# Four pieces, not three, of the next GEMM begun inside the layer norms of a one-core transformer kernel, and another order of the last norm

## The chip, the cores and the metric

One core of a Trainium2 chip. The metric is the device time of one execution in microseconds, median of several runs. The engines are TensorE (PE in the profile, its weight loads PEld), VectorE (DVE), ScalarE (ACT), GpSimd (POOL) and SyncE (SP), which here only issues transfers.

## The reference

A block of one mixture layer is followed by two post-norm layers, 512 tokens by 1024 features, in float32. The change lies in the layer norms of the latter:

```
def layernorm(x, g, b):
    mu = mean(x); var = mean((x - mu) ** 2)
    return (x - mu) * rsqrt(var + LN_EPS) * g + b

def hybrid_layer(x, ...):                  # twice
    ...                                    # fox attention and retention -> mixed
    x = layernorm(ALPHA * x + mixed @ w_out, ln1_g, ln1_b)
    hid = square(relu(x @ w_ff1))
    return layernorm(ALPHA * x + hid @ w_ff2, ln2_g, ln2_b)
```

So there are four norms. Norms 1 and 3 (the first of each layer) are followed by the GEMM with w_ff1, norm 2 by the projections of the second layer (w_in), norm 4 by the output.

## The kernel before, in words

Activations lie transposed: features on the 128 partitions in 8 tiles k, the 512 tokens along the free axis. H holds the residual stream. Each GEMM operand is split into a high and a low part (Phi and Plo, Qhi and Qlo, wh and wl), and each product is three matmuls: high by high (L298), low by high (L300), high by low (L301). A GEMM of one piece (128 output features) is 8 tiles k, 24 matmuls of 512 columns, or twice 24 of 256 columns where it is done by token halves. Results go to PSUM banks 0 to 3 in turn; the norms' sums use banks 4 and 5.

**Weights.** A slab of two pieces is loaded by SyncE (L229) into one of two stages. prepare() takes the next piece and splits it: ScalarE writes the high part (L269), VectorE the low part (L270), into a slot of a ring: slots 0 to 3, and after widen() also 4 to 6, which lie over buffers that attention uses; narrow() gives these back. When both pieces of a stage are split, the next slab's load is issued. piece() hands out the next piece and prepares ahead; piece(1) prepares nothing more than it needs.

**Order.** Every engine has one in-order queue, written by V.op (VectorE), A.op (ScalarE), PE.op and SP.op in program order. An op waits for the tokens that it is given; a token is a count of its engine's semaphore, so a wait for an op is also one for all that stands before it in that queue.

**The norm.** Norm.tile(j) adds tile j of H to accq (L1164) and, against a rough centre cB, takes deviations (L1180), squares (L1187) and their sum acc2 (L1196). The last three tiles, 5 to 7, are made by last_three() in two token halves, A_ (tokens 0 to 255) and B_ (256 to 511). part(p, hf, ks) does the matmuls of tile 5+p for half hf; if ks ends with 7 it evacuates them (L1273, or L1277 without the factor alpha) and calls norm.late(j, sl): add to accq (L1202), whose token becomes norm.acc, and deviate(). norm.add() adds pending squares.

For each half, mean() is a float32 matmul of accq with a matrix of 1/1024 (L1217, two matmuls), a copy by ScalarE into muB (L1219), and the difference to cB and its square (L1220, L1221). minus(k) subtracts muB (L1226). scale() is a matmul of acc2 (L1231), the variance (L1233), and ln and exp on ScalarE (L1235, L1236). times(k) multiplies by rB (L1241), lets ScalarE apply gain and bias (L1244) and, if a GEMM follows, write Phi (L1247); lows(k) writes Plo (L1253). head(half, ks) does the matmuls of the next GEMM's first pieces, each on its bank, tile by tile as they come.

The order before is: tiles 5, 6 and 7 of half A; 9 matmuls of tile 5's half B; A's mean; 6 matmuls; A's scale; 9 matmuls; tile 6's and tile 7's half B, with A's times() and lows() put between; then the head with three pieces for half A, with B's mean and scale inside, and for half B. Two pieces are prepared ahead of half B's head. Behind the head the three banks are evacuated, and the GEMM goes on with its fourth piece. In norm 2 the pieces are those of fq0, fk0 and fq1, evacuated by Heads.queries (L602, L603) and keys (L617, L618); the fourth, fk1, is a GEMM of its own, and a thin GEMM of 8 output features (gemm_thin) follows it. In norm 4 no GEMM follows: out_half() has SyncE write finished tiles to the output, four at a time for half A (512 KB), two for half B (256 KB).

## Time and profile before

| | |
|---|---|
| Runs | 2123.3, 2123.97, 2124.76 us; median 2123.97 |
| The profiled execution | 2123.57 us |
| Its span, first to last instruction | 2121.8 us |
| Mean granted clock of TensorE | 0.995 |
| Norm 1, from tile 5 to the end of its head | 1089 to 1132 us |
| Norm 2 | 1449 to 1491 us |
| Norm 3 | 1728 to 1772 us |
| Norm 4, to the end | 2089 to 2122 us |

Every time in the views is in us from the span's start, for this one execution. In a timeline a row is an instruction, or several of the same line in a row (x3), with start and duration; in brackets stands the time for which its engine had nothing to do before it, and what released it. Durations of one engine's instructions overlap: of 256-column ones on VectorE each takes 0.42 us. A matmul's shape such as 128x256 gives the columns.

### The profile page before, as it was taken

To read this page: it belongs to the slowest core of one execution; us is meant where nothing else is said; L and a number is where in the kernel's file an instruction comes from. 1 tells how busy PE (TensorE), PEld (TensorE's weight loads), DVE (VectorE), ACT (ScalarE), POOL (GpSimd) and SP (SyncE) were. 2 spreads that over 40 slices of the span, in tenths; PEclk is the share of its full clock that TensorE was granted. 3 is DMA by queue.
4 is the path that set the end of the run, shared out by engine and by line. 5 is a ranking of instruction groups with operands and counts; after the bars stand their busy time and mean duration, and the time that the engine had idled before them with its cause. 6 is when DMAs were issued, how large, how long until landed. Compare 5 with 4: busy or idle time off the path is not lost. (4 is left out here: it accounts for less than half of the span.)

```text
span 2121.8 us, 24498 instructions
## 1 busy us (share of the span) xinstructions
PE 2055.1 (97%) x9660; PEld 1691.6 (80%) x9660; DVE 1101.9 (52%) x1795; ACT 939.3 (44%) x1513; POOL 149.4 (7%) x207
## 2 busy tenths in 40 slices
PE   8999999999999999999999999999999999999997
PEld 6888778888888888777688888888777688888886
DVE  5655556565343443576486333337676476333336
ACT  5664334335232332565557243244565347243343
POOL 0000000000000000353000000000353000000000
PEclk9999999999999999999999999999999999999999
DMA  7332213333322332632323332330632323333321
GB/s 236 95 105 64 77 60 99 121 98 120 119 91 88 100 99 61 179 100 75 114 80 102 99 103 95 100 99 21 199 91 83 114 80 100 100 99 100 99 80 40
DMA packets 201519, 211.38 MB, mean 100 GB/s; under 512 B 7803, under 2 KB 181115, under 8 KB 201404
## 3 DMA queue, kind: packets, MB, share of 16 engines
q1 hardware_dynamic: 194544, 194.13, 29.2%
q0 software_dynamic: 6352, 15.24, 2.8%
q8 instruction: 77, 1.26, 0.3%
q10 hardware_dynamic: 508, 0.43, 0.1%
q14 instruction: 38, 0.31, 0.0%
HBM read 194.55 MB, written 8.95 MB: 96 GB/s over the span
## 5 line engine op out<-in xcount | busy, mean ns | idle before, releaser
L298 PE MATMUL ps<-Phi,wh 128*128 128x512 f32 (+1 forms) x1208 | 481.1, 398 | 18.9 <-DVE Plo L448 8.7
L301 PE MATMUL ps<-Phi,wl 128*128 128x512 f32 (+1 forms) x1208 | 459.3, 380 | 0.1
L300 PE MATMUL ps<-Plo,wh 128*128 128x512 f32 (+1 forms) x1208 | 458.4, 380 | 0.0
L269 ACT ACTIVATE wh<-stage 128x1024 fp32r<-128x1024 f32 (+2 forms) x253 | 261.5, 1041 | 183.9 <-PE ps L301 167.1
L270 DVE TENSOR_TENSOR wl<-stage,wh 128x1024 fp32r<-128x1024 f32 x250 | 304.6, 1223 | 66.2 <-ACT wh L269 58.5
L298 PEld LDWEIGHTS ps<-Phi,wh 128*128 128x128 f32 x1208 | 228.4, 189 | 67.0 <-issue 19.6
L301 PEld LDWEIGHTS ps<-Phi,wl 128*128 128x128 f32 x1208 | 227.7, 188 | 44.7 <-DVE wl L270 0.8
L300 PEld LDWEIGHTS ps<-Plo,wh 128*128 128x128 f32 x1208 | 228.5, 189 | 40.8 <-issue 4.1
L298 PE MATMUL ps<-Qhi,wh 128*128 128x512 f32 (+1 forms) x680 | 256.2, 377 | 0.8 <-DVE Qlo L445 0.8
L301 PE MATMUL ps<-Qhi,wl 128*128 128x512 f32 (+1 forms) x680 | 254.4, 374 | 0.0
L300 PE MATMUL ps<-Qlo,wh 128*128 128x512 f32 (+1 forms) x680 | 254.4, 374 | 0.0
L445 DVE TENSOR_TENSOR Qlo<-f,Qhi 128x512 fp32r<-128x512 f32 x96 | 66.5, 693 | 238.8 <-ACT Qhi L444 238.8
L1120 DVE TENSOR_TENSOR H<-H,ps 128x512 f32<-128x512 f32 x72 | 49.5, 687 | 222.6 <-PE ps L301 222.6
L298 PE MATMUL ps<-Qhi,wxh 128*128 128x512 f32 (+1 forms) x408 | 150.7, 369 | 0.0
L300 PE MATMUL ps<-Qlo,wxh 128*128 128x512 f32 (+1 forms) x408 | 148.9, 365 | 0.0
L301 PE MATMUL ps<-Qhi,wxl 128*128 128x512 f32 (+1 forms) x408 | 148.8, 365 | 0.0
L298 PEld LDWEIGHTS ps<-Qhi,wh 128*128 128x128 f32 x680 | 128.1, 188 | 25.3 <-ACT Qhi L444 1.6
L300 PEld LDWEIGHTS ps<-Qlo,wh 128*128 128x128 f32 x680 | 128.1, 188 | 23.6 <-issue 1.0
L301 PEld LDWEIGHTS ps<-Qhi,wl 128*128 128x128 f32 x680 | 128.0, 188 | 22.7
L269 ACT ACTIVATE wxh<-stage 128x1024 fp32r<-128x1024 f32 x86 | 89.7, 1051 | 109.2 <-PE ps L301 104.3
L298 PE MATMUL ps<-Phi,wxh 128*128 128x512 f32 (+1 forms) x336 | 129.0, 384 | 0.0
L300 PE MATMUL ps<-Plo,wxh 128*128 128x512 f32 (+1 forms) x336 | 129.0, 384 | 0.0
(301 smaller groups left out, 2921.5 us busy)
## 6 DMA issues: line engine op xcount, KB each, us to landing
stage<-in_w_ff SPq DMA_DIRECT2D x64, 1024.0 KB, 5.4
stage<-in_w_in SPq DMA_DIRECT2D x39, 1024.0 KB, 5.3
stage<-in_w_up SPq DMA_DIRECT2D x16, 1024.0 KB, 5.3
stage<-in_w_down SPq DMA_DIRECT2D x16, 1024.0 KB, 5.2
stage<-in_w_in SPq DMA_DIRECT2D x30, 512.0 KB, 5.3
stage<-in_w_out SPq DMA_DIRECT2D x12, 1024.0 KB, 5.2
stage<-in_w_bg SPq DMA_DIRECT2D x4, 1024.0 KB, 5.4
vrev<-H SPq DMA_DIRECT2D x2, 2048.0 KB, 14.9
```

Source lines behind the costliest of these rows:

```text
L269: t_hi = A.op(lambda e: e.activation(hi, src, ACT.Copy), st_landed[n, part], w_free[u], sem=s_whi)
L270: t_lo = V.op(lambda e: e.tensor_tensor(lo, src, hi.bitcast(F32), ALU.subtract), st_landed[n, part], t_hi, w_free[u], sem=s_wlo)
L298: PE.op(lambda e: e.matmul(o, hi[:, k, c], x.hi[:, kx, tok], start=first, stop=False), t_hi, t_x or x.t[kx], list(waits), signal=False)
L300: PE.op(lambda e: e.matmul(o, hi[:, k, c], x.lo[:, kx, tok], start=False, stop=False), signal=False)
L301: return PE.op(lambda e: e.matmul(o, lo[:, k, c], x.hi[:, kx, tok], start=False, stop=last), t_lo, sem=s_wpe, signal=last)
L445: t2 = V.op(lambda e: e.tensor_tensor(lo, src, hi.bitcast(F32), ALU.subtract), t1, t_src, x.free, after)
L1120: t_h[j] = V.op(lambda e: e.tensor_tensor(H[:, j, :], H[:, j, :], o, ALU.add), t, t_h[j])
```

## The change

In last_three():

- The fourth piece of the next GEMM is prepared right behind tile 7's half A and norm.add(), and the head has four pieces. narrow() comes after it.
- A's mean comes after all of tile 5's half B (24 matmuls), A's scale after 4 of 8 tiles k of tile 6's half B. times(), lows() and minus() of both halves are dealt out anew.
- Half B's head goes tile by tile over the four pieces up to k = 3, then piece by piece over k = 4 to 7. If last_wide is not set, each bank is evacuated behind its piece; with last_wide (norm 2) all four are evacuated behind the last product.
- The GEMM goes on with its fifth piece: ff() begins at 4, and in norm 2 the thin GEMM follows at once.
- In norm 4, tile 7's half B is not added to accq and acc2. mean(7) and scale(True) let TensorE add it, by a second float32 matmul into the same bank each. Of times(), tiles 2 and 5 get gain and bias from VectorE (tensor_scalar) and not from ScalarE. B's operations are woven into A's, and A's last tile is finished later.

```diff
-            def late(self, j, sl):
+            def late(self, j, sl, summed=True):
-                self.acc = V.op(lambda e: e.tensor_tensor(accq[:, sl], accq[:, sl], H[:, j, sl], ALU.add),
-                                t_h[j], self.acc)
+                if summed:
+                    self.acc = V.op(lambda e: e.tensor_tensor(accq[:, sl], accq[:, sl], H[:, j, sl], ALU.add),
+                                    t_h[j], self.acc)
                 self.deviate(j, sl)
...
-            def mean(self):
+            def mean(self, rest=None):
...
+                if rest is not None:
+                    t = PE.op(lambda e: e.matmul(banks[4][:, sl], onec[:, :], H[:, rest, sl], start=False, stop=True),
+                              t_h[rest])
...
-            def scale(self):
+            def scale(self, rest=False):
...
+                while rest and n.pending:
+                    _, _, s, t_s = n.pending.pop()
+                    t = PE.op(lambda e, s=s: e.matmul(banks[5][:, sl], onec[:, :], s[:, sl], start=False, stop=True), t_s)
...
+                    if not self.keep and k in (2, 5):
+                        self.fin[k] = V.op(lambda e, k=k, g=g, b=b: e.tensor_scalar(
+                            H[:, k, sl], d8[:, k, sl], g, b, ALU.mult, ALU.add), t)
+                        continue
...
-                norm.late(j, sl)
+                norm.late(j, sl, then)
...
+            part(2, 0, range(8))
+            norm.add()
+            if nxt:
+                prepare()
             if last_wide:
                 narrow()
-            part(2, 0, range(8))
-            norm.add()
-            part(0, 1, range(3))
+            part(0, 1, range(8))
             A_.mean()
             A_.minus(0, 1, 2, 3)
-            part(0, 1, (3, 4))
+            part(1, 1, range(4))
             A_.scale()
             A_.minus(4, 5, 6, 7)
-            part(0, 1, (5, 6, 7))
+            part(1, 1, range(4, 8))
             A_.times(0, 1)
+            if not nxt:
+                norm.add()
+                part(2, 1, range(8), False)
+                A_.times(2, 3)
+                B_.mean(7)
+                B_.minus(0)
+                B_.scale(True)
+                A_.times(4)
+                B_.minus(1, 2, 3, 4, 5)
+                A_.times(5, 6)
+                B_.minus(6, 7)
+                B_.times(0)
+                A_.times(7)
+                out_half(0, A_.fin)
+                for k in range(1, 8):
+                    B_.times(k)
+                    out_half(1, B_.fin, k)
+                return
             A_.lows(0)
-            part(1, 1, range(8))
-            for k in range(2, 5):
-                A_.times(k)
-                A_.lows(k - 1)
+            A_.times(2)
+            A_.lows(1)
+            A_.times(3)
             part(2, 1, range(8))
             norm.add()
+            A_.lows(2)
+            A_.times(4)
...
+            four = [(piece(1), next_bank()) for _ in range(4)]
...
             head(A_, (0, 1))
+            A_.lows(3)
+            A_.times(5)
             B_.mean()
-            A_.times(5)
             A_.lows(4)
-            B_.minus(0, 1)
+            B_.minus(0, 1, 2)
+            A_.times(6)
+            A_.lows(5)
             head(A_, (2, 3))
             B_.scale()
-            A_.times(6)
-            A_.lows(5)
-            B_.minus(2, 3, 4)
+            B_.minus(3, 4)
             A_.times(7)
-            A_.lows(6, 7)
+            A_.lows(6)
+            B_.minus(5, 6, 7)
+            A_.lows(7)
             head(A_, (4, 5, 6, 7))
...
+            head(B_, range(4))
+            for ((i, w), b), ev in zip(four, nxt):
+                for k in range(4, 8):
+                    t = step(B_, k, i, w, b)
+                P.free = t
+                release(i, t)
+                if not last_wide:
                     free[b] = ev(banks[b][:, :], t)
+            for ((i, w), b), ev in zip(four, nxt if last_wide else ()):
+                free[b] = ev(banks[b][:, :], t)
```

## Rows read from the trace of the kernel before

**Rows 1.** The page, busy time, share of the span and instructions of each engine.

```profile
PE 2055.1 (97%) x9660; PEld 1691.6 (80%) x9660; DVE 1101.9 (52%) x1795; ACT 939.3 (44%) x1513; POOL 149.4 (7%) x207
```

**Rows 2.** Waits of TensorE: line, for what, us in total, times, longest.

```profile
PE ps L1217 <- DVE accq L1202: 8.9, 6, 2.1
...
PE ps L298 <- ACT H L1244: 4.7, 3, 1.6
...
PE ps L298 <- DVE Plo L1253: 3.1, 8, 0.6
```

**Rows 3.** Timeline, TensorE, norm 1: start, us, what, [idle before <-releaser].

```profile
1098.18 0.28 PE L298 MATMUL ps<-Qhi,wxh 128*128 128x256 f32 x1
...
1100.28 0.70 PE L1217 MATMUL ps<-accq,onec 128*128 128x256 f32 x2 [0.86 <-DVE accq L1202]
...
1113.58 0.70 PE L1217 MATMUL ps<-accq,onec 128*128 128x256 f32 x2 [1.55 <-DVE accq L1202]
...
1123.92 0.35 PE L298 MATMUL ps<-Phi,wh 128*128 128x256 f32 x1 [1.58 <-ACT H L1244]
```

**Rows 4.** Timeline, ScalarE and VectorE, norm 1.

```profile
1100.60 0.42 ACT L1187 ACTIVATE sq<-d 128x256 f32<-128x256 f32 x1 [1.62 <-DVE d L1180]
...
1106.37 0.60 ACT L1244 ACTIVATE H<-d,prm 128x256 f32<-128x256 f32 x1
...
1088.65 3.50 DVE L270 TENSOR_TENSOR wl<-stage,wh 128x1024 fp32r<-128x1024 f32 x3
...
1101.78 1.42 DVE L1226 TENSOR_TENSOR d<-H,muB 128x256 f32<-128x256 f32 x4
```

**Rows 5.** Stretches: from:to, busy us (matmuls) of PE first, PEclk third from last.

```profile
222.00:226.00 4.00, 1.60 (x9) 1.06 (x8) 3.54 (x6) 1.25 (x3) 0.00 (x0) 1.00 0.11 8
...
1620.00:1627.00 7.00, 2.01 (x9) 1.44 (x9) 4.97 (x11) 3.05 (x6) 3.15 (x4) 1.00 0.00 0
...
1739.80:1743.30 3.50, 3.50 (x13) 3.14 (x13) 2.60 (x8) 1.22 (x3) 0.00 (x0) 0.51 0.00 0
```

**Rows 6.** Timeline, VectorE and TensorE, norm 3, first mean.

```profile
1737.71 1.22 DVE L270 TENSOR_TENSOR wl<-stage,wh 128x1024 fp32r<-128x1024 f32 x1 [0.59 <-ACT wh L269]
1738.85 0.41 DVE L1273 SCALAR_TENSOR_TENSOR H<-H,ps 128x256 f32<-128x256 f32 x1
...
1739.78 1.16 PE L1217 MATMUL ps<-accq,onec 128*128 128x256 f32 x2 [2.09 <-DVE accq L1202]
```

**Rows 7.** Timeline, norm 2: a square, the end of its head, evacuations, a split.

```profile
1459.16 0.42 ACT L1187 ACTIVATE sq<-d 128x256 f32<-128x256 f32 x1 [1.88 <-DVE d L1180]
...
1491.06 0.28 PE L301 MATMUL ps<-Phi,wxl 128*128 128x256 f32 x1
1491.18 0.40 PE L298 MATMUL ps<-Phi,wh 128*128 128x512 f32 x1
...
1496.66 0.40 PE L333 MATMUL ps<-Phi,wh 128*40 128x512 f32 x1
...
1492.01 1.41 DVE L603 SCALAR_TENSOR_TENSOR f0qs<-ps,f0qs 64x512 fp32r<-64x512 f32 x2 [0.99 <-ACT f0qs L602]
...
1496.33 1.06 ACT L269 ACTIVATE wh<-stage 128x1024 fp32r<-128x1024 f32 x1 [1.26 <-DMA stage<-in_w_in]
```

**Rows 8.** Timeline and DMA, norm 4; last, one line's instructions (ns min/median/max).

```profile
2108.18 0.42 DVE L1277 TENSOR_TENSOR H<-H,ps 128x256 f32<-128x256 f32 x1
...
2114.63 2.77 DVE L1241 TENSOR_TENSOR d<-d,rB 128x256 f32<-128x256 f32 x8
...
2115.08 4.04 ACT L1244 ACTIVATE H<-d,prm 128x256 f32<-128x256 f32 x8 [0.74 <-DVE d L1241]
...
out_T<-H SPq DMA_DIRECT2D x2, 512.0 KB, 3.0
out_T<-H SPq DMA_DIRECT2D x4, 256.0 KB, 2.2
...
L875 DVE TENSOR_SCALAR x_z<-x_z,prm x2: 474/474/475, 868.3 to 1505.0; 8x512 f32<-8x512 f32 x2
```

More of the change, by code:

```diff
@@ L1213, in __init__ @@
                 self.y, self.fin, self.sub = {}, {}, {}
-            def mean(self):
+            def mean(self, rest=None):
                 sl, n = self.sl, self.n
-                t = PE.op(lambda e: e.matmul(banks[4][:, sl], onec[:, :], accq[:, sl], start=True, stop=True),
+                t = PE.op(lambda e: e.matmul(banks[4][:, sl], onec[:, :], accq[:, sl], start=True, stop=rest is None),
                           n.acc, free[4])
+                if rest is not None:
+                    t = PE.op(lambda e: e.matmul(banks[4][:, sl], onec[:, :], H[:, rest, sl], start=False, stop=True),
+                              t_h[rest])
                 self.t_m = free[4] = A.op(lambda e: e.activation(muB[:, sl], banks[4][:, sl], ACT.Copy), t, n.start)
@@ L1227, in minus @@
                                      self.t_m, t_h[k], self.n.d[k])
-            def scale(self):
+            def scale(self, rest=False):
                 sl, n = self.sl, self.n
-                t = PE.op(lambda e: e.matmul(banks[5][:, sl], onec[:, :], acc2[:, sl], start=True, stop=True),
+                t = PE.op(lambda e: e.matmul(banks[5][:, sl], onec[:, :], acc2[:, sl], start=True, stop=not rest),
                           n.acc2, free[5])
+                while rest and n.pending:
+                    _, _, s, t_s = n.pending.pop()
+                    t = PE.op(lambda e, s=s: e.matmul(banks[5][:, sl], onec[:, :], s[:, sl], start=False, stop=True), t_s)
                 t = V.op(lambda e: e.tensor_tensor(qB[:, sl], banks[5][:, sl], qB[:, sl], ALU.subtract), t, self.q)
@@ L1302, in last_three @@
             A_.lows(0)
-            part(1, 1, range(8))
-            for k in range(2, 5):
-                A_.times(k)
-                A_.lows(k - 1)
+            A_.times(2)
+            A_.lows(1)
+            A_.times(3)
             part(2, 1, range(8))
             norm.add()
-            if nxt:
-                two = [(piece(1), next_bank()) for _ in range(3)]
-            def head(half, ks):
-                for k in ks if nxt else ():
-                    for (i, w), b in two:
-                        t = product(banks[b][:, half.sl], w, k, slice(0, 128), P, k, k == 0, k == 7, free[b],
-                                    tok=half.sl, t_x=half.sub[k])
-                        if k == 7 and half is B_:
-                            P.free = t
-                            release(i, t)
-                return t if nxt else None
+            A_.lows(2)
@@ L1322, in last_three, with step @@
+            A_.times(4)
+            four = [(piece(1), next_bank()) for _ in range(4)]
+            def step(half, k, i, w, b):
+                return product(banks[b][:, half.sl], w, k, slice(0, 128), P, k, k == 0, k == 7, free[b],
+                               tok=half.sl, t_x=half.sub[k])
+            def head(half, ks):
+                for k in ks:
+                    for (i, w), b in four:
+                        step(half, k, i, w, b)
             head(A_, (0, 1))
+            A_.lows(3)
@@ L1337, in last_three @@
-            B_.minus(5, 6, 7)
             B_.times(0)
@@ L1341, in last_three @@
                 B_.lows(k - 1)
-                if nxt is None:
-                    out_half(1, B_.fin, k)
             B_.lows(7)
-            if nxt:
-                prepare()
-                prepare()
+            prepare()
+            prepare()
             for k in range(8):
                 t_h[k] = [A_.fin[k], B_.fin[k]]
-                P.t[k] = [A_.sub.get(k), B_.sub.get(k)]
+                P.t[k] = [A_.sub[k], B_.sub[k]]
             rb_free[0] = B_.r
             sq_free[:] = [norm.acc2, norm.acc2]
-            if nxt:
-                t = head(B_, range(8))
-                for (_, b), ev in zip(two, nxt):
+            head(B_, range(4))
[5 more added lines that the diff above has]
+                if not last_wide:
                     free[b] = ev(banks[b][:, :], t)
+            for ((i, w), b), ev in zip(four, nxt if last_wide else ()):
+                free[b] = ev(banks[b][:, :], t)
         fring = [pair_ring("f0", g0 + 54), pair_ring("f1", g0 + 28)]
@@ L1622, in build @@
             last_three(norm, alpha, V_LN1G + 8 * L, V_LN1B + 8 * L,
-                       [lambda o, t, j=j: up(j, o, t) for j in range(3)])
+                       [lambda o, t, j=j: up(j, o, t) for j in range(4)])
             norm = None
-            for j in ff(up, alpha, 3, 5):
+            for j in ff(up, alpha, 4, 5):
                 if norm is None:
```

6 lines of the change are left out of this document (2 added, 4 removed).

## The prediction

> **What bounds the kernel now.** I read the page first: TensorE is busy for 2055.1 of 2121.8 us [rows 1], so only time in which it waits can be won, and every new wait is paid in full. The waits of TensorE, longest first, show what the four norms cost it [rows 2]: 8.9 us before the mean sums (L1217), 4.7 us before the second half's first GEMM products, 3.1 us in eight waits of at most 0.6 for low parts of P in the first half's head. The timeline of norm 1 places the long ones [rows 3]: 0.86 us before the first half's mean at 1100.28, 1.55 before the second half's at 1113.58, 1.58 before the second half's head at 1123.92. Start to start each is some 0.2 us longer; with three of the eight norm 1 loses 6.2 us. Norms 2 and 3 repeat it: norm 2 has no first wait, norm 3 has 2.09 us there [rows 6], after a weight split on VectorE. Norm 4 ends the kernel.
>
> Reading VectorE and ScalarE [rows 4], the norm is a chain on two in-order queues. Four VectorE operations of 256 columns take 1.42 us, so one passes every 0.335 us; an operation that needs the one before it starts 0.45 us after it. A weight split takes ScalarE 1.06 us [rows 7] and holds VectorE for 1.14 us a piece (three in 3.50). A 256-column matmul passes every 0.119 us, a 512-column one every 0.228 (24 from 1491.18 to 1496.66) [rows 7].
>
> **Part 1, order around the first half's mean, norms 1 to 4.** Before, A_.mean() stands behind 9 products of the second half of tile 5. Now it stands behind all 24 and their late(). late() evacuates that half and adds it to accq, and norm.acc then names this later add. The matmul of A_.mean() waits for norm.acc, so it now waits for a sum that it doesn't need. Before those two VectorE operations stands the new prepare(). By hand, norm 1: the last square of half A starts at 1100.60 [rows 4]; the ScalarE split follows 0.33 later and takes 1.05; VectorE's split starts at 1102.0 and passes in 1.14; evacuation 0.45 and add 0.43 end at 1104.0, mean at 1104.1. TensorE has been free since 1098.18 + 24 x 0.119 = 1101.0 [rows 3]. The wait grows from 1.1 to 3.1 us. Norm 2 by the same steps from its square at 1459.16 [rows 7]: mean at 1462.6 against TensorE free at 1460.6, 2.1 us where there was none. Norm 3, from its mean at 1739.78 and so 3.8 later: 4.2 us [rows 6]. Norm 4 has no prepare(): mean at 2101.8, 1.2 us.
>
> **Part 2, the fourth piece in the head.** A's mean at 1104.1 gives VectorE its first input 1.15 later, as now from 1100.28 to one operation before 1101.78 [rows 3, 4]. Mean and variance step and 8 subtractions are 10 x 0.335: 1108.6. Tile 6 takes 2.0 (evacuation 0.45, add, deviation and two sums 4 x 0.335, 0.2 for ScalarE's square): 1110.6. Then times 0.45, ScalarE's scale-and-shift 0.63, its copy 0.45, low part 0.43, and 0.14 until TensorE starts: the first product of head A at 1112.7. TensorE arrives at 1104.1 + 0.53 + 0.53 (mean and variance matmuls) + 48 x 0.119 = 1110.8. That is a wait of 1.9 us where there was 0.8. Head A then has 96 products (11.4 us) in place of 72. It covers the second half's chain nearly: the 1.8 before B's mean goes, and of the others (0.4, 0.6, 1.8) I get 0.3, 0.1, 0.3, 0.3 within head A and 0.4 before head B, by passing the new order through the two queues with these durations. Sum of norm 1: waits 6.2 before, 3.1 + 1.9 + 1.4 = 6.4 after; half B's head ends at 1137.8, against 1123.92 + 72 x 0.119 = 1132.5 and 5.5 more for the piece that was a GEMM of its own. The half-width products cost 48 x 0.119 against 24 x 0.228, 0.2 more, and are in it. The same order applied to the old kernel gives 6.6 of waits where the trace has 6.2, so the change of norm 1 is -0.4 to +0.4; I take -0.1. Norms 2 and 3 have the same queue work and come out the same, -0.2 each. The fourth split is no new work: it moves from the end of the head, where VectorE waited for ScalarE at every tile, to where VectorE is the limit, and that is what eats the gain. It also issues the next slab's load on SyncE some 29 us earlier; SyncE's queue holds nothing else there and the other stage is full already, so nothing waits for it. Behind norm 2 the split at 1496.33, which waited 1.26 us for its load, is no longer on a load's heels [rows 7]; TensorE did not wait for it, so that is worth 0. Without the moved split these steps give 1.1 (norm 2) to 1.9 us gained.
>
> VectorE as a strict queue is the rule that speaks against this place. The trace shows it in norm 3: the split at 1737.71 holds back the evacuation at 1738.85, which needs nothing of it [rows 6]. The Trainium skill, "TensorE: Matmul & The Clock Gate", section "Architectural detail", says that ScalarE and VectorE are strict first-in first-out; by that rule the evacuation behind the moved split can't pass it, and the trace agrees.
>
> **Part 3, the clock.** In norm 3 the granted clock fell behind the wait: 0.51 from 1739.8 to 1743.3, which is 1.2 GHz, and 13 matmuls ran there, where 3.5 us hold 29 at 0.119 [rows 5]. It fell likewise behind 1620 to 1627, with TensorE busy 2.01 of 7 us, and not behind the 2.4 us without work near 222 us. Norm 1's new 3.1 us lie among these cases, norm 3's 4.2 beyond them. A fall costs nothing to 1.7 us (half of 3.4); half of it is covered, since head A waits for VectorE anyway, but mean, tile 6 and its evacuation come later. I take 1.1 for norm 1, and 0.9 for norm 3, whose old fall cost little (it lay on VectorE's chain). Norm 2 at 2.1: nothing taken, 1.2 as the upper bound.
>
> **Part 4, the bank behind norm 2.** Before, fq0, fk0 and fq1 were evacuated behind the head while a GEMM of 24 full products on the fourth bank ran: the last head product started at 1491.06 and the next at 1491.18 [rows 7]. Now all four banks are in the head, last_wide evacuates behind its last product, and the thin GEMM comes next, on fq0's bank. It waits for two ScalarE copies, and for two VectorE operations that end at 1492.01 + 1.41 = 1493.42 [rows 7]; TensorE would go on at 1493.55, 2.35 us late. Nothing else stands there to cover it. Bounds: 0, were another bank next in the round of four, and 3.1, were one more 0.7 us operation ahead on VectorE. In norms 1 and 3 the evacuations go out piece by piece in the head: 0. The head's new order needs half B's tile 7 after 4 x 12 + 9 products, 6.8 us; low parts come every 0.95 us, the last after 6.6: 0 as well, 0.3 at most.
>
> **Part 5, the last norm.** Half B's last tile is ready at 2101.8 + 0.53 + 0.53 + 48 x 0.119 + 0.2, evacuated at 2108.9, 0.7 later than now [rows 8]. Then mean(7)'s copy stands on ScalarE behind A_.times(3), which VectorE reaches after deviation, times(2), its new tensor_scalar and times(3), at 2110.5: copy at 2111.4, variance on VectorE at 2112.8. Behind it stand 22 VectorE operations before the last times, 22 x 0.335 and three dependent steps at 0.12 more: 2120.5, against 2114.63 + 7 x 0.335 = 2116.97 now. Three of A's times that now stand before the last evacuation come after it, and four scale-and-shifts join VectorE (ScalarE's 8 of 4.04 us are then no longer the limit, VectorE is). Last scale-and-shift ends 2121.7 against 2119.12: +2.6. Output: A's second 512 KB go out at 2118.5, not 2114.4, so 1536 KB leave from there; 512 KB land 3.0 and 256 KB 2.2 us after their issue [rows 8], so each 256 KB takes 0.8 or a little less and 1.4 is latency: 4.6 + 1.4, 2124.5, against 2119.15 + 2.2. So +2.6 to +3.1. The new tensor_scalar has no row at 128 x 256; bounds 0.24 (half of the 8 x 512 one of 474 ns) and 0.42 (a tensor_tensor of that width); that 8 x 512 one, with a column of prm, is the nearest in kind; it took 474 ns, where full-width tensor_tensors take 0.7 [rows 7], so some 0.3, and I take +2.8.
>
> For that operation the Trainium skill, "VectorE: DVE Perf Modes", section "Walkthrough: the 8-slice pipeline in each mode", says that fp32 tensor_scalar between SBUF tiles makes two results a cycle. With its 151 fixed cycles at 0.96 GHz an estimate from that page is 0.29 us, and the tail would be +2.7. The row of 474 ns agrees in kind; no run here shows the form itself.
>
> **Sum.** Norm 1: -0.1 + 1.1; norm 2: -0.2 + 2.35; norm 3: -0.2 + 0.9; norm 4: +2.8. Together +6.65, from the profiled execution's 2123.57 (span 2121.8, 1.8 around it) to 2130.2. The median of the runs is 0.4 above that execution: 2130.5.
>
> **Rivals.** (a) The clock falls too in norm 2 or behind the bank wait: +1.2 and +1.7. For it: 2.09 us sufficed in norm 3. Against: 2.4 us near 222 us did not. 2132 to 2133.5. (b) The moved split is covered: if VectorE had idle time there, norms 1 to 3 would gain 1.9, 1.1 and 1.9 and with the tail and the bank come to +0.25: 2124.2, no difference. Against: its operations follow each other without a gap there, as at 1101.78 [rows 4]. (c) Faster: the place is B's mean and B's head. If both lose their waits, 1.8 and 1.8 in three norms, and A's mean is not held back, -10.8 against +5.15 for bank and tail gives 2118.3; it decides if head A's first product comes less than 0.8 us after TensorE is free. Against: part 1's token. (d) The tail alone turns, as ScalarE's 4.04 us of scale-and-shifts fall by a quarter: -1.0 in place of +2.8, 2126.7.
>
> **How the numbers follow.** Forecast 0.62 (2127.5 to 2132, with (d) at its edge); (a) 0.18; (b) 0.12; (c) 0.08. 0.2%, about what a measurement of this kernel can tell from no change, is 4.2 us: under 2119.8 faster, over 2128.2 slower. Faster 0.06; same 0.16, which is (b) and the low edge of the forecast; slower 0.78. The range leaves out (c), most of (b) and the far end of (a): 2125.5 to 2133.5.
>
> **What would show it.** In the new profile: idle before L1217 near 3, 2, 4 and 1 us, released by an accq add of the second half, with one VectorE split ahead of it; head A's first product 1.5 to 2.3 us late; near nothing before B's mean; a wait of 2 to 2.5 us of the thin GEMM's first product on a VectorE evacuation; two falls of the clock in norms 1 and 3; from last evacuation to last scale-and-shift 12.8 us, now 10.9. Wrong if A's mean starts with no wait, if the B-half waits stay, or if the tail after the last GEMM product is not longer.

## The result: 0.46% slower, and the profile of the changed kernel

Median of five runs 2133.84 us (2131.38 to 2135.22) against 2123.3 us for the kernel before on the same chip. The ratio of the means (2133.35 and 2123.68) is 1.0046, with a 95% interval of 1.0031 to 1.006. The profiled execution took 2131.38 us, the shortest of the five, with a span of 2129.5 us and a mean granted clock of 0.993 (before: 0.995).

The page, busy time by engine, and TensorE's waits (line, for what, us, times, longest):

```profile
PE 2059.9 (97%) x9736; PEld 1696.9 (80%) x9736; DVE 1102.3 (52%) x1797; ACT 936.0 (44%) x1509; POOL 149.5 (7%) x207
```

```profile
PE ps L1219 <- DVE accq L1203: 9.7, 4, 4.1
...
PE ps L298 <- ACT H L1256: 5.1, 3, 1.8
...
PE ps L333 <- DVE f0qs L603: 2.2, 1, 2.2
```

TensorE has 76 instructions more than in [rows 1] and is busy 4.8 us more, and the span is 7.7 longer. The 8.9 us before the mean sums [rows 2] are now 9.7, but in 4 waits of up to 4.1 where there were 6 of up to 2.1: all stand before half A's mean, none before B's. The eight waits for low parts of P (0.2 to 0.6 us each) have gone from the list. The three for ScalarE's H (L298, 4.7 us then) stood before head B and now stand before head A, and the thin GEMM (L333) has a new one.

TensorE's timeline, the long waits of norm 1 (mean, head A), norm 2 (mean), the thin GEMM behind it, norm 3 and norm 4 (mean):

```profile
1100.47 0.28 PE L301 MATMUL ps<-Qhi,wxl 128*128 128x256 f32 x1
1103.58 0.70 PE L1219 MATMUL ps<-accq,onec 128*128 128x256 f32 x2 [2.83 <-DVE accq L1203]
...
1112.23 0.36 PE L298 MATMUL ps<-Phi,wh 128*128 128x256 f32 x1 [1.78 <-ACT H L1256]
...
1462.02 0.70 PE L1219 MATMUL ps<-accq,onec 128*128 128x256 f32 x2 [1.88 <-DVE accq L1203]
...
1498.28 0.62 PE L333 MATMUL ps<-Phi,wh 128*40 128x512 f32 x1 [2.21 <-DVE f0qs L603]
...
1747.58 0.80 PE L1219 MATMUL ps<-accq,onec 128*128 128x256 f32 x1 [4.06 <-DVE accq L1203]
...
2106.23 0.70 PE L1219 MATMUL ps<-accq,onec 128*128 128x256 f32 x2 [0.97 <-DVE accq L1203]
```

What stands before the first of them, VectorE's timeline:

```profile
1100.56 0.42 DVE L1196 TENSOR_TENSOR acc<-acc,sq 128x256 f32<-128x256 f32 x1 [0.48 <-ACT sq L1187]
1101.51 1.23 DVE L270 TENSOR_TENSOR wxl<-stage,wxh 128x1024 fp32r<-128x1024 f32 x1 [0.52 <-ACT wxh L269]
1102.65 0.41 DVE L1285 SCALAR_TENSOR_TENSOR H<-H,ps 128x256 f32<-128x256 f32 x1
1103.10 0.42 DVE L1203 TENSOR_TENSOR accq<-accq,H 128x256 f32<-128x256 f32 x1
```

The last product of tile 5's second half starts at 1100.47; half A's last add was over before that. The mean starts at 1103.58, right behind the add at 1103.10, which is half B's and which it doesn't need. Ahead of that add stands the moved split (1101.51, passed by 1102.65).

Stretches (from:to, busy us and matmuls of PE first, PEclk third from last):

```profile
1103.00:1106.00 3.00, 2.42 (x17) 2.31 (x18) 2.10 (x7) 1.22 (x3) 0.00 (x0) 1.00 0.61 182
1497.90:1501.30 3.40, 3.02 (x8) 1.35 (x9) 3.25 (x6) 3.26 (x7) 2.64 (x5) 0.51 1.05 389
1624.20:1634.40 10.20, 6.93 (x22) 5.26 (x20) 4.99 (x9) 2.33 (x5) 0.46 (x1) 0.50 0.01 2
1747.10:1750.50 3.40, 2.92 (x11) 2.75 (x12) 2.01 (x6) 1.22 (x3) 0.00 (x0) 0.50 0.70 218
```

The clock kept its upper level, 2.4 GHz, behind norm 1's wait of 2.83 us. It fell to 1.2 GHz behind the thin GEMM's wait and behind norm 3's, and at 1624.2, in the retention part, it stayed low for 10.2 us; the kernel before had 3.4 us there, at 1627.2.

The end (VectorE, ScalarE, output DMA, and one line's instructions with ns min/median/max):

```profile
2113.44 0.42 DVE L1289 TENSOR_TENSOR H<-H,ps 128x256 f32<-128x256 f32 x1
...
2114.69 0.41 DVE L1253 TENSOR_SCALAR H<-d,prm 128x256 f32<-128x256 f32 x1
2115.01 0.42 DVE L1249 TENSOR_TENSOR d<-d,rB 128x256 f32<-128x256 f32 x1
...
2124.73 0.75 DVE L1249 TENSOR_TENSOR d<-d,rB 128x256 f32<-128x256 f32 x2
...
2115.98 0.36 ACT L1224 ACTIVATE muB<-ps 128x256 f32<-128x256 f32 x1
...
2125.18 1.09 ACT L1256 ACTIVATE H<-d,prm 128x256 f32<-128x256 f32 x2 [0.36 <-DVE d L1249]
...
out_T<-H SPq DMA_DIRECT2D x2, 512.0 KB, 3.0
out_T<-H SPq DMA_DIRECT2D x4, 256.0 KB, 3.2
...
L1253 DVE TENSOR_SCALAR H<-d,prm x4: 414/414/414, 2114.7 to 2124.4; 128x256 f32<-128x256 f32 x4
```

From the last evacuation (2113.44) to the end of the last scale-and-shift (2125.18 + 1.09) it takes 12.83 us; [rows 8] give 10.94. The output's last 256 KB are there 2.85 us after that, 2.24 before. The new tensor_scalar takes 414 ns and lets the next operation pass after 0.32 (2114.69 to 2115.01), as a tensor_tensor of that width does.

One more row, from the retention part (TensorE):

```profile
1670.12 0.95 PE L1582 MATMUL ps<-x_rqk 128*128 128x256 f32 x4 [1.74 <-DVE x_IT L1585]
```

It waits for VectorE, and VectorE for a load of decay factors (x_dec). The load landed 12.0 us after its issue, 10.9 before. The same place in the kernel before, and a wait of that kernel between the thin GEMM and norm 3 that has all but gone in the changed one (no wait over 0.3 us for x_fvv is left):

```profile
1525.17 0.47 PE L298 MATMUL ps<-Phi,wh 128*128 128x512 f32 x1 [1.40 <-DVE x_fvv L773]
...
1666.12 0.95 PE L1547 MATMUL ps<-x_rqk 128*128 128x256 f32 x4 [0.64 <-DVE x_IT L1550]
```

Set beside the trace of before, stretch by stretch: up to the end of norm 1's fourth piece -0.65 us; on to the thin GEMM's start +2.26; on to norm 3 +2.42; in norm 3 +0.44; from there to the end +3.28. Together +7.75. The third of them, matmul by matmul: the fall behind the bank wait +1.39; then -1.68, at that wait for x_fvv; the low clock at 1624 +1.56; the load +1.11.

Of the first -0.65, norm 1 has only -0.17. These are its first half-width product and the first full-width one behind its head, in the kernel before and in the changed kernel:

```profile
1089.55 0.28 PE L298 MATMUL ps<-Qhi,wxh 128*128 128x256 f32 x1
1138.09 0.39 PE L298 MATMUL ps<-Phi,wxh 128*128 128x512 f32 x1
...
1089.08 0.28 PE L298 MATMUL ps<-Qhi,wxh 128*128 128x256 f32 x1
1137.45 0.40 PE L298 MATMUL ps<-Phi,wxh 128*128 128x512 f32 x1
```

That is 48.54 and 48.37 us. The other 0.47 lies ahead of norm 1, where both kernels do the same.

### The profile page after: what moved, and what is told of

Its sections match the earlier page's. It is cut to its first block and busy times, and to the rows that moved or that the text cites. A ratio compares the mean times of both kernels' runs of the same rounds, so it can differ in the third digit from the quotient of the medians.

```text
span 2129.5 us, 24654 instructions
## 1 busy us (share of the span) xinstructions
PE 2059.9 (97%) x9736; PEld 1696.9 (80%) x9736; DVE 1102.3 (52%) x1797; ACT 936.0 (44%) x1509; POOL 149.5 (7%) x207
## 5 line engine op out<-in xcount | busy, mean ns | idle before, releaser
L298 PE MATMUL ps<-Phi,wh 128*128 128x512 f32 (+1 forms) x1200 | 477.3, 398 | 15.3 <-DVE Plo L448 9.0
L298 PEld LDWEIGHTS ps<-Phi,wh 128*128 128x128 f32 x1200 | 227.0, 189 | 64.4 <-issue 24.1
L298 PE MATMUL ps<-Qhi,wh 128*128 128x512 f32 (+1 forms) x680 | 256.9, 378 | 0.8 <-DVE Qlo L445 0.8
L298 PE MATMUL ps<-Qhi,wxh 128*128 128x512 f32 (+1 forms) x408 | 149.8, 367 | 0.0
L298 PEld LDWEIGHTS ps<-Qhi,wh 128*128 128x128 f32 x680 | 128.0, 188 | 25.2 <-ACT Qhi L444 1.6
L300 PE MATMUL ps<-Plo,wxh 128*128 128x512 f32 (+1 forms) x368 | 136.4, 371 | 0.0
L298 PE MATMUL ps<-Phi,wxh 128*128 128x512 f32 (+1 forms) x368 | 136.4, 371 | 0.0
## 6 DMA issues: line engine op xcount, KB each, us to landing
vrev<-H SPq DMA_DIRECT2D x2, 2048.0 KB, 12.8
```

The costliest lines, as they stand in the source:

```text
L298: PE.op(lambda e: e.matmul(o, hi[:, k, c], x.hi[:, kx, tok], start=first, stop=False), t_hi, t_x or x.t[kx], list(waits), signal=False)
L300: PE.op(lambda e: e.matmul(o, hi[:, k, c], x.lo[:, kx, tok], start=False, stop=False), signal=False)
```

## The experiments

Theory: the order around A's mean and the split ahead of it (part 1), VectorE's queue (part 2), the clock (3), the bank (4) and the tail (5) add up as predicted. Rivals are named with each run. They were measured in four groups, each on a chip of its own with the kernel before beside it (medians 2122.9 to 2124.0); a ratio is that of the means of 5, 11 or 12 runs of a version and of the kernel before in its own group.

**1. Is the late token or the queue the limit?** A's mean is told to wait for its own half's sum alone:

```
             norm.add()
+            own = norm.acc
...
-            A_.mean()
+            A_.mean(acc=own)     # the matmul waits for own, not norm.acc
```

> Changed kernel, but A's mean waits for the accq add of its own half only. Theory (VectorE's queue sets norms 1 to 3, the needless wait is only where the time shows): the 3.0, 2.0 and 4.2 us before A's mean go and come back before head A's first product (some 4.9, 3.9, 5.6 us there), total within 1 us of the changed kernel's 2133.8, since VectorE has the same work in the same order. Norm 4 within 0.2 us. Rival (the needless wait is the cost itself): all three waits and 1.1 us in norm 4 are won, 2123.5 to 2125.

2132.68 us, 1.0035 [1.0021, 1.0049], which is 1.2 us below the changed kernel where "within 1" was expected, and far from the rival's 2125. TensorE and VectorE of norm 1:

```profile
1103.82 0.60 PE L1219 MATMUL ps<-accq,onec 128*128 128x256 f32 x2
...
1115.33 0.55 PE L298 MATMUL ps<-Phi,wh 128*128 128x256 f32 x1 [4.75 <-ACT H L1256]
...
1104.73 1.23 DVE L270 TENSOR_TENSOR wxl<-stage,wxh 128x1024 fp32r<-128x1024 f32 x1 [0.53 <-ACT wxh L269]
```

No wait is left before the mean at 1103.82, and head A's first product waits 4.75 us instead of 1.78. The two waits of before (3.0 and 1.9, start to start) came together in one (4.9). The waits for head A in norms 2 and 3 grew likewise, to 3.81 and 5.45. From the first half-width product to the end of the head's pieces norms 2 and 3 took 49.9 and 50.5 us, 49.8 and 50.7 in the changed kernel. So the token costs next to nothing: VectorE's queue, with the split in it, sets when head A can begin.

**2. The tail, taken out and put in alone.** Norm 4 in the order of before, all gains and biases on ScalarE, in the changed kernel; and the reverse, norm 4 of the change in the kernel before:

```
+            if not nxt:
+                part(0, 1, range(3)); A_.mean(); ...      # norm 4 as before
```

> Changed kernel with norm 4 in the order of before, all gains and biases on ScalarE. Theory (the new last norm has 5 more operations on VectorE behind the last evacuation and starts 0.7 us later): 2.8 to 3.3 us less than the changed kernel, 2130.7 median. Rival (the tail is set by ScalarE and the output's transfers either way): within 0.5 us of 2133.8. Rival 2 (the new tail is a gain and norms 1 to 3 lose all): 2135 or more.

> Edit: the kernel before with the change's norm 4 alone; norms 1 to 3 are the kernel before. Theory (part 5: the new order puts B's mean copy and the 22 VectorE operations behind it late): from the last evacuation to the last scale-and-shift 12.8 us instead of 10.9, the end 2.8 to 3.3 us later than the kernel before, 2126 to 2127, ratio 1.0013 to 1.0016. Rival (d, the quarter of the scale-and-shifts that goes to VectorE turns it): 2122 to 2123.5, no slower than the kernel before.

Old tail: 2129.68 us, 1.0025 [1.0016, 1.0034]. New tail alone: 2128.09 us, 1.0017 [1.0008, 1.0026]. By medians these are 4.2 us less than the changed kernel and 4.7 more than the kernel before, where 2.8 to 3.3 was expected of both; the traces give 3.2 for each. The latter's last evacuation and last scale-and-shifts:

```profile
2107.39 0.42 DVE L1288 TENSOR_TENSOR H<-H,ps 128x256 f32<-128x256 f32 x1
...
2119.13 1.09 ACT L1255 ACTIVATE H<-d,prm 128x256 f32<-128x256 f32 x2 [0.36 <-DVE d L1248]
```

12.83 us again (2107.39 to 2120.22), and from the end of norm 3's fourth piece to the end of the span 3.24 us more than before. From its first half-width product to the end, norm 4 takes 32.7 us with the old tail, 35.9 with the new one. Rival (d) is out.

**3. The thin GEMM on a bank of its own (bank 7).**

```
-            ev_fl(zf, gemm_thin(P, zf, t_ph))
+            ev_fl(zf, gemm_thin(P, zf, t_ph, 7 if L else None))   # bank
```

> Changed kernel, but the thin GEMM behind norm 2 goes to bank 7, which is free, so it need not wait for fq0's evacuation. Theory: the 2.4 us before it go and the fall of the clock behind them with it (1.7 us where it happened): 2.4 to 4.1 less than the changed kernel, 2129.7 to 2131.4. Rival (the wait moves to the next GEMM's banks or to the attention behind): within 0.5 us of 2133.8.

2135.78 us, 1.0052 [1.004, 1.0065]. The bank wait is gone, and this stands behind it:

```profile
1515.35 0.41 PE L1463 MATMUL ps<-cst,x_cs 8*128 8x8 f32 x4 [2.40 <-DVE x_cs L1451]
```

The transposes of cs (L1463) wait 2.4 us for the scan, whose inputs stand behind the evacuations on VectorE. So the theory failed, and the rival was right in kind: the bank is only where VectorE's backlog shows first. The median is 2 us above even the rival's 2133.8, though. Up to the thin GEMM norm 2 won 2.2 us; from there to behind the transposes TensorE lost 4.1 against the kernel before, as the clock fell to 1.2 GHz behind their wait too (3.4 us from 1516.6), where the changed kernel lost 1.4.

**4. The split's low part on GpSimd instead of VectorE.**

```
-            t_lo = V.op(lambda e: e.tensor_tensor(lo, src, hi..., ALU.subtract), ...
+            t_lo = (low or V).op(...)          # prepare(G) for the moved split
```

> Changed kernel, but the low part of the moved fourth piece is written by GpSimd, not VectorE; ScalarE's half stays where it is. Theory (the moved split's 1.14 us and its wait for ScalarE are on VectorE's chain): waits before A's mean 1.2, 1.1, 2.3 us, 1.8 + 0.9 + 1.8 less in norms 1 to 3 and fewer falls of the clock, 2127.5 to 2129.3. GpSimd has 9 us for it; rival (GpSimd takes over 9 us, or slows VectorE): wait before head A's first product grows, 2134 or more. Rival 2 (order alone costs, the split is covered): within 1 us of 2133.8.

2135.72 us, 1.0052 [1.004, 1.0065]: the theory's 2127.5 to 2129.3 failed, and the first rival (GpSimd slows VectorE) held. GpSimd and VectorE in norm 1:

```profile
1104.18 2.40 POOL L270 TENSOR_TENSOR wxl<-stage,wxh 128x1024 fp32r<-128x1024 f32 x1 [116.68 <-ACT wxh L269]
...
1104.26 2.60 DVE L1180 TENSOR_TENSOR d<-H,cB 128x256 f32<-128x256 f32 x1
```

GpSimd took 2.40 us, and the VectorE subtraction that started 0.08 behind it took 2.60 instead of 0.42: it ended 0.28 after GpSimd's. VectorE lost 2.2 us where the split itself had cost it 1.14. The Trainium skill, "SBUF — State Buffer", section "SBUF: two separate sides", says that a VectorE operation with two SBUF inputs and a GpSimd one that reads SBUF take a shared port pair in turns, each for its whole length; the trace agrees. Head A's first product then waited 4.0 us in norms 1 and 3. In norm 2 the operation that ran beside GpSimd's was the add that A's mean waits for (2.04 us instead of 0.42), so that this wait was 2.7 us where 1.1 was expected.

**5. Four pieces, order of before.** Norms 1 to 3 keep the four-piece head and the moved split; the order around A's mean and in head A is the old one, and norm 4 too.

> Edit: norms 1 to 3 keep four pieces in the head and the fourth split where the change put it, but the order of the kernel before around A's mean, in head A and in norm 4 is back. Theory (the order in parts 1 and 5 costs the time; the wide head itself gives a little back, the bank wait takes 2.35): waits before A's mean fall back to 1.1, 0 and 2.1 us in norms 1 to 3, the wait of the thin GEMM's first product stays at 2.3 to 2.4 us, norm 4 is as before; norms 1 to 3 gain 0.2 each over the kernel before: 2125.5 to 2127, 1.0008 to 1.0014 times the kernel before. Rival (the wide head itself, four pieces in place of three, costs the time, not the order): 2130 or more, with B's waits or new waits in head A showing it.

2126.51 us, 1.0017 [1.0008, 1.0026]; 2125.5 to 2127 was expected. TensorE in norm 1, and the thin GEMM:

```profile
1101.02 0.70 PE L1219 MATMUL ps<-accq,onec 128*128 128x256 f32 x2 [0.84 <-DVE accq L1203]
...
1110.45 0.35 PE L298 MATMUL ps<-Phi,wh 128*128 128x256 f32 x1 [0.67 <-ACT H L1256]
...
1113.15 0.36 PE L298 MATMUL ps<-Phi,wh 128*128 128x256 f32 x1 [1.04 <-DVE Plo L1265]
...
1116.00 0.70 PE L1219 MATMUL ps<-accq,onec 128*128 128x256 f32 x2 [1.18 <-DVE accq L1203]
...
1499.41 0.40 PE L333 MATMUL ps<-Phi,wh 128*40 128x512 f32 x1 [2.21 <-DVE f0qs L603]
```

A's mean waits as before, the bank wait is there, and a wait of 1.04 in head A is new, presumably as the split pushes the low parts back. Against number 2's 2129.68 (same tail, new order) the old order is 3.2 us less, of which the section on the clock leaves 0.5 at equal clock. The new order takes B's waits away and pays with A's; it is nearly even in the queues, and worse in the clock. What the moved split costs by itself isn't measured: no run has the new order without it.

**6. The clock.** The changed kernel with matmuls nobody reads in TensorE's waits:

```
+            for _ in range(many):               # 22, 14, 30, 7 in norms 1 to 4
+                PE.op(lambda e: e.matmul(banks[7][:, 0:256], tail[2][1][0][:, 0, 0:128], Q.hi[:, 0, 0:256], ...
             A_.mean()
...                                          # and 13, 13, 11 before head A, 10 before the thin GEMM
```

> Edit: the changed kernel, with matmuls that nobody reads put into TensorE's waits (22, 14, 30 and 7 of 256 columns before A's mean in norms 1 to 4, 13, 13 and 11 before head A, 10 of 512 columns before the thin GEMM behind norm 2); each filling is shorter than the wait that it stands in. Theory (part of the slowdown is that the granted clock falls behind the new waits): the granted clock no longer falls in or behind the norms and behind the bank wait; the waits themselves stay as long as they were, minus the filling; 2 to 5 us faster than the changed kernel, 2129 to 2132. Rival (the clock is of no account, the waits are all of it): no difference, 2133 to 2136 beside 2124 for the kernel before, or slower by what the filling overshoots.

2131.34 us, 1.0032 [1.002, 1.0044]. TensorE of norm 1, and stretches:

```profile
1106.48 0.70 PE L1223 MATMUL ps<-accq,onec 128*128 128x256 f32 x2 [0.18 <-DVE accq L1207]
...
1115.13 0.35 PE L299 MATMUL ps<-Phi,wh 128*128 128x256 f32 x1 [0.22 <-ACT H L1260]
...
1101.00:1106.50 5.50, 5.32 (x46) 5.11 (x44) 4.28 (x10) 1.76 (x3) 0.00 (x0) 1.00 0.00 0
1502.60:1506.00 3.40, 3.40 (x16) 2.12 (x15) 3.27 (x5) 2.29 (x4) 2.59 (x6) 1.00 1.06 398
1748.70:1752.00 3.30, 3.30 (x24) 3.19 (x25) 2.43 (x8) 1.24 (x4) 0.00 (x0) 1.00 0.83 267
1626.30:1636.50 10.20, 6.93 (x20) 5.15 (x19) 4.63 (x9) 2.32 (x5) 0.61 (x2) 0.50 0.00 0
```

Behind norm 3 and the bank wait the clock now stays at its upper level; half A's chain in norm 1 is as long as ever (head A's first product comes 8.65 us after the mean, as in the changed kernel). The fall at 1626 is there, as long as in the changed kernel. So some 2.5 us of the 10.5 are the clock's in the norms and behind the bank wait. That is by two medians of five runs each, whose intervals (1.002 to 1.0044 and 1.0031 to 1.006) overlap. One place can be read directly: from norm 3's first mean to the end of its fourth piece it takes 33.87 us here, as norm 1 does in both versions, and 34.99 in the changed kernel. The fall there cost 1.1 us.

**7. Half-A products where TensorE waits.** The kernel before, with the fourth piece split behind B's last subtraction and its half-A products as a stretch of 24 between the heads, in norms 1 and 3:

```
             B_.minus(5, 6, 7)
+            if wide:
+                prepare()
+                fourth = piece(1), next_bank()
+                for k in range(8):
+                    step(A_, k, *fourth[0], fourth[1])
             B_.times(0)
```

> Edit: the kernel before, in norms 1 and 3 with a fourth piece, but split behind B's minus(5, 6, 7), its half-A products as a stretch of 24 of its own behind head A and before head B, and half B's head over four pieces. Order around both means, norm 2 and norm 4 are the kernel before. Theory (half-A products are good only where VectorE is the later one and its queue is not lengthened ahead of them; here they cover the 1.8 us before head B): the wait before head B's first product falls from 1.6 to 1.8 us to under 0.3 in norms 1 and 3, no other wait grows, 1.5 us less in each: 2120.5 to 2121.5, 0.9986 times the kernel before. Rival (the split there holds back B's times and low parts on VectorE, so that the wait moves into head B): no difference, 2123 to 2125, with waits between head B's products.

2122.6 us, 0.9997 [0.9988, 1.0005]. TensorE in norm 1:

```profile
1113.85 0.70 PE L1217 MATMUL ps<-accq,onec 128*128 128x256 f32 x2 [1.55 <-DVE accq L1202]
...
1123.34 0.39 PE L301 MATMUL ps<-Phi,wxl 128*128 128x256 f32 x1 [0.50 <-DVE wxl L270]
```

The 1.58 before head B [rows 3] is gone; 0.50 for the late low part of the weight is new. From A's mean to the end of the fourth piece 37.0 us, 37.8 before: 0.8 instead of the 1.5 expected. Norm 3 in this profile won nothing (50.6 us from its first half-width product to the end of the fourth piece, 50.3 before): the clock fell behind B's mean wait of 1.54. Number 8's norm 3, the same code with the fall behind A's mean, took 49.0. The time isn't distinguishable from the kernel before, where 2120.5 to 2121.5 was expected.

**8. The best of it.** Number 7, and in norm 4, in the old order, B's mean and variance take the last tile by a second matmul each, with one gain-and-bias (tile 3 of B) on VectorE:

```
-            B_.mean()
+            B_.mean(None if nxt else 7)
...
-            B_.scale()
+            B_.scale(not nxt)
```

> Edit: the previous one, and in norm 4, in the order of the kernel before, B's mean and variance take the last tile by a second matmul each (the change's rest), and one of B's gain-and-bias operations (tile 3) is on VectorE. Theory (of the new last norm the second matmuls and a little work on VectorE are sound, what costs is the order that puts A's copy and times behind): from the last evacuation to the last scale-and-shift 10.2 us instead of 10.9; 0.7 us less than the previous one, 2120 to 2121, 0.9983 times the kernel before. Rival (the tail is bound by VectorE's count of operations, so that the tensor_scalar costs what the matmuls gain): no difference from the previous one.

2121.62 us, 0.9991 [0.9982, 0.9999], above the 2120 to 2121 expected. The last evacuation to the last scale-and-shift: 10.30 us, 10.2 expected.

**9. Three attempts to get the rest.** Number 8 with the weight's low-part products last in the stretch, and norm 2 with a fourth piece; the same with norm 3's split behind tile 7's first half; and the low-part products alone:

```
-                for k in range(8): step(A_, k, *fourth[0], fourth[1])
+                for k in range(8): ...hi x P.hi, hi x P.lo
+                for k in range(8): ...lo x P.hi
```

> Edit: the previous version with the late fourth piece (norms 1 and 3) and the tail, and two things more: in the fourth piece's half-A stretch the 8 products with the weight's low part come last, and norm 2 has the fourth piece (fk1) too, its half-B products behind the heads of the other three, whose evacuations they cover (24 x 0.119 = 2.9 us against the 2.3 to 2.4 of the bank wait). Theory: the 0.66 us wait for the low part goes in norms 1 and 3, the 1.7 us before head B in norm 2 goes and the thin GEMM's first product doesn't wait: 1.3 and 1.7 us, 2118 to 2119.5, 0.9975 times the kernel before. Rival (the evacuations of norm 2, now 2.7 us closer to each other and to the thin GEMM's, delay the chain behind it, as they did in the run with the thin GEMM on another bank): 2120 to 2121.5, with a wait near the cs transposes behind the thin GEMM.

> Edit: the same, and the loop that splits the weights missing by A's mean (one split, in norm 3 alone) stands behind tile 7's first half instead of in front of it. Theory (VectorE is strictly in order, the split is what holds back A's mean in norm 3): the wait before A's mean there falls from 2.2 us to 0.2 to 0.5, and 0.9 to 1.7 come back at head A's first products; the end of norm 3 is 0.1 earlier by the queues, and 0 to 0.9 more where the clock no longer falls behind the wait: 0.1 to 1 us less than the previous one. Rival (any split among those steps costs the same): no difference.

> Edit: the version with the late fourth piece in norms 1 and 3 and the tail (norm 2 as in the kernel before), with one thing more: in the fourth piece's half-A stretch the 8 products with the weight's low part come last. It is the step that the last two versions had in common, without their norm 2. Theory (norm 2's early fk1 moves a wait behind the thin GEMM and costs clock there, the low part's order is sound): the 0.66 us wait goes in norms 1 and 3, 2120 to 2121, 0.9985 times the kernel before. Rival (once the waits are this short, what is taken from them comes back as a lower granted clock, wherever it is taken): mean clock 0.994 in place of 0.995 and 2122 to 2123, no faster than the version without it.

2122.73 us, 0.9996 [0.9987, 1.0005]; 2123.23 us, 0.9996 [0.9988, 1.0005]; 2121.55 us, 0.9991 [0.9982, 1.0]. The 0.5 us wait is gone in all three, and in the first two the wait before head B in norm 2; but none is clearly faster than number 8, and all miss the times expected of them. The first has a new wait behind the thin GEMM, for a weight's low part, and the second has norm 3's mean wait moved to head A's first products in part (0.27 and 0.74 us for the 2.09 of before). Norm 3 takes 48.3 us in it, without a fall of the clock, against 48.7 in the first and 48.3 in the third with one, and that little doesn't show in the medians:

```profile
1502.71 0.50 PE L375 MATMUL ps<-wl,Phi 128*128 128x512 f32 x1 [0.65 <-DVE wl L270]
```

```profile
1738.28 0.70 PE L1218 MATMUL ps<-accq,onec 128*128 128x256 f32 x2 [0.27 <-DVE accq L1203]
...
1747.79 0.36 PE L298 MATMUL ps<-Phi,wh 128*128 128x256 f32 x1 [0.74 <-ACT H L1255]
```

Why the first wins nothing can be read in its profile: norm 2 gains the 1.45 us up to the thin GEMM that were expected, loses 1.16 up to 1530 (the new wait, and x_fvv's, which grew to 1.63) and 3.0 at 1669, where the load of x_dec landed 12.4 us after its issue and a fall of the clock stood beside it. The rival of a chain behind norm 2 was right in kind, though the wait is another than it named.

## The clock over all runs

The mean granted clock of one kernel differs from run to run. The kernel before at 0.996 took 2123.0 us (mean of 27 runs), at 0.995 2123.5 (43), at 0.992 2127.7 (8). I fitted one line for every kernel with a common slope over 200 runs: 0.26 us for each us at the lower level (time there worked out as 2 x (1 - clock) x time; the records give the clock to 0.001, so the slope is if anything too flat). It parts each kernel's distance from the kernel before, in means, into what is left at equal clock and what the clock's difference makes:

| kernel | at equal clock | clock | runs |
|---|---|---|---|
| the change | +6.4 | +3.0 | 5 |
| 1, own sum | +3.6 | +5.0 | 5 |
| 2, old tail | +2.3 | +3.1 | 11 |
| 2, new tail alone | +2.9 | +0.8 | 11 |
| 3, thin bank | +6.4 | +5.0 | 5 |
| 4, GpSimd | +5.7 | +5.7 | 5 |
| 5, old order | +1.7 | +1.6 | 12 |
| 6, filled | +6.3 | +0.5 | 5 |
| 7, late fourth | -2.0 | +1.0 | 11 |
| 8, with the tail | -1.5 | -0.4 | 11 |
| 9, low part last | -2.5 | +0.4 | 11 |
| 9, norm 2 too | -1.9 | +1.2 | 11 |
| 9, split behind | -1.9 | +1.3 | 11 |

With the residual of 1.1 us a run, 5 runs fix a term to some 0.5 and 11 to 0.35. Filling the waits takes 2.5 us of clock away and leaves the rest as it was, which supports the split by an intervention. Number 1 speaks against trusting it further: its norms are as long as the changed kernel's in the traces, yet its term at equal clock is 2.8 lower and its clock term 2.0 higher. One slope for all may charge too much for a fall that lies where TensorE waits for VectorE anyway; that isn't shown.

Number 7 is 2.0 ahead at equal clock and loses half of it to the clock. How far such terms can be trusted shows in number 8, whose trace has a tail 0.64 us shorter than number 7's and whose term is 0.5 worse; and so whether the low-part order (-2.5, clock +0.4) is better than number 8, or the clock takes back what it wins, is left open.

Nor is the rule of the clock settled. What decides whether it falls behind a given wait stays open: norm 1's 2.83 us did not bring it down in the changed kernel's profile, its 2.82 in number 2's did (0.50 from 1106.9 on), and norm 3's 2.09 did in the kernel before [rows 5] but not in number 7, whose norm 3 begins alike (1.00 from 1737.2 on, then 0.50 from 1750.5 on behind B's mean), and nowhere in norm 3 in number 5 (2.08 there).

## Why the prediction was right, and where it was off

The forecast was 2130.5 us in 2125.5 to 2133.5, with slower at 0.78. The sign and the mechanism held; the median came out 3.3 us above, and so 0.3 above the range, which was too narrow at its upper end. The profiled executions differ by 7.8 against the 6.65 of the sum, which is 1.2 of the 3.3. The rest is that the changed kernel's median lies 2.5 above its profiled execution, where the forecast had added 0.3 for that. That the profiled sum comes so near is in part luck: norm 1 came to -0.17 instead of +1.0, as the fall there didn't come in this profile, 0.47 went ahead of norm 1, and between the thin GEMM and norm 3, where the prediction had nothing, four terms (+1.39, -1.68, +1.56, +1.11) made +2.4.

**Part 1 right.** Forecast 3.1, 2.1, 4.2 and 1.2 us before A's mean; measured, start to start, 2.99, 2.04, 4.22 and 1.13. Number 1 adds what the prediction had only in part 2: without the token all of it comes back at head A.

**Part 2 right, as far as it is tested.** Head A's first product: forecast 1.9 late, measured 1.94, 1.95 and 1.71. B's waits: no wait before B's mean, 0.36 and 0.27 as the longest in norm 1's head. Norm 1 as a whole: forecast -0.1 without the clock, measured -0.17, with no fall there in this profile; norm 2 with its bank +2.2 against -0.2 + 2.35. The 1.1 to 1.9 us that the steps give for the moved split alone stay an estimate, as no run takes only it away. VectorE as a strict queue ("TensorE: Matmul & The Clock Gate", section "Architectural detail" of the Trainium skill) held in the rows above, where the evacuation at 1102.65 starts as the split at 1101.51 lets it.

**Part 3, the term mis-sized.** It had 1.1 in norm 1 and 0.9 in norm 3, and nothing elsewhere. In the profile norm 1 had no fall. Norm 3 had one in both kernels: the new one costs 1.1 (number 6), the old one 0.5 by the same measure (38.31 us from its first mean where norms 1 and 2 have 37.81), and norm 3 came to +0.44, near the forecast's -0.2 + 0.9. The clock cost 1.39 behind the bank wait, which was rival (a), and 1.56 in the retention part at 1624, which no part of the change touches. Over the five runs the fit gives the clock +3.0 of the difference in means, where the prediction had 2.0, all read from a single profile in which a fall is partly chance.

**Part 4 right at its place, not in its effect.** 2.35 forecast, 2.37 measured. But "Nothing else stands there to cover it" looked 2 us ahead and not 30: the 1.40 us wait for x_fvv, in the same trace, took back what norm 2 and the fall had cost there, 1.68 in the changed kernel and 1.28 in number 5. And the lower bound "0, were another bank next" was wrong: in number 3, on another bank, the wait came back at the transposes.

**Part 5 nearly right.** +2.8 forecast, +3.28 in the profile and +3.24 alone. Last evacuation 0.8 later (0.7 forecast), 12.83 us from there (12.8), the output's end 0.6 more. The sum had +2.6 to +3.1, and 2.8 was taken for the tensor_scalar's sake at 0.3 us: it took 0.414. So the choice of 0.3 from the 8 x 512 row was wrong, within its bounds (0.24 and 0.42). The rule on fp32 tensor_scalar in "VectorE: DVE Perf Modes", section "Walkthrough: the 8-slice pipeline in each mode" of the Trainium skill, whose estimate was 0.29, isn't borne out for this shape: its instructions of 128 x 256 pass as slowly as tensor_tensors do.

**Rivals.** (a) came true behind the bank wait and not in norm 2's first wait, in this profile. (b) would have needed the moved split to be covered: number 1's wait of 4.75 us behind it says that it wasn't. (c) is out by part 1, and number 1 shows that even without the token it fails. (d) fell with number 2. What (c) had in mind, half-A products to cover a wait, works where VectorE isn't lengthened ahead of half A: number 7 is as fast as the kernel before and its B wait is gone; number 8 is 0.09% faster, with an interval that ends just short of 1 and as one of five such attempts, so it is hardly shown to be a gain.

## What to carry to other kernels

Before moving work of an in-order engine to cover a wait of another, ask which engine is late at the new place: behind half B's subtractions the same split costs TensorE a wait of 0.5 us (number 7), and in front of half A's mean it stands on the chain that sets the pace. A token that names more than is needed is worth a look, but here taking it away moved the wait to the next thing that the queue released, and another bank did likewise. And where waits are a microsecond or two, judge kernels over many runs with the granted clock beside the time, since one profile shows one draw of it.

## What was not expected of the hardware

A GpSimd tensor_tensor of 128 x 1024 fp32 took 2.40 us, and the VectorE tensor_tensor beside it 2.60 instead of 0.42, so that the offload cost VectorE twice what it took away (number 4). A tensor_scalar of 128 x 256 fp32 with two parameter columns takes 414 ns, as long as a tensor_tensor of that size, while the one of 8 x 512 took 474 where full-width tensor_tensors take 0.7 us [rows 7, 8]. And the clock: the kernel before took 2121.6 to 2129.5 us over 86 runs beside the experiments, with a clock of 0.996 to 0.991. The load of x_dec landed 10.3 to 12.4 us after its issue over all the traces, with nothing changed in it.
